# Latent attention steps of a two-layer transformer kernel issued in pairs of opposite order

## The chip, the cores and the metric

One Trainium2 chip, one of its cores. The time is the device time of one execution in microseconds (us). An execution of the kernel before takes 1641.88 us (median of three runs, 1641.62 to 1645.02). Everything is float32 unless a tile is an index, a mask (bfloat16) or a half-precision helper.

## The reference, cut to what matters

Two layers work on 256 latent tokens and 256 context tokens of width 1024. Each layer has three attention branches of eight heads with 64 values each, then a merge through gates, an output projection and a mixture of 16 experts. The change touches the attention alone:

```python
# branch A (global), B (window of +-128 with a sink logit), N (2-D neighbourhood with a bias)
s = q . [k_latent, k_context] * 64 ** -0.5      # (+ band mask in B, + position bias in N)
p = softmax(s)                                  # B adds one sink logit to the sum
o = p . [v_latent, v_context]
# context queries see context keys only, and are needed in layer 0 alone
```

## The kernel before

**Tiles and stages.** A layer projects its normalised tokens to queries, keys and values, runs the attention, merges the three branches through gates, projects, and routes to the experts. The engines have their instruction streams written out by hand and meet through counting semaphores. There is no planner for the attention: the order on each engine is the order in which its loop issues.

**The attention's unit is a pair of heads.** `att_pairs(l)` lists (branch, query tile of 128 tokens, pair of heads), branch outermost and pair innermost: 3 branches x 4 tiles x 4 pairs = 48 in layer 0 (tiles 0 and 1 latent, 2 and 3 context) and 3 x 2 x 4 = 24 in layer 1 (latent only). So layer 0 alternates between 8 latent pairs and 8 context pairs, three times, and layer 1 has 24 latent pairs in a row. A latent pair attends to 512 keys, a context pair to 256. For pair d:

- **S(d), scores** (L2048): for each of the two heads ("sides") one matmul of 64 rows by 128 columns over 512 keys (256 for context), into one of four score banks. The trace records each as two matmuls, and the two sides run side by side on halves of the array's rows.
- **M(d), row maxima** on VectorE, one for each side: L1405 for branch A and for context, L1410 for B (adds the band mask and writes the sum to `probs`), L1417 for latent N (adds the position bias that GpSimd made at L756 from a table that SyncE's queue loads at L612).
- **E(d), exponentials** on ScalarE, one for each side (L1039), into `probs`, a ring of six = three pairs. Each is followed by a short read of the accumulated sum.
- **R(d), reciprocal and normalisation** on VectorE (L1389, L1391).
- **T(d), transposes** on TensorE (L2019): 128x128 blocks of `probs`, four for each side of a latent pair (two for context), into banks 3 and 4.
- **C(d), copies** on ScalarE (L1022) of the transposed blocks to `PT`, which has two buffers (in tiles WK and MB).
- **V(d), values** on TensorE (L2038): `PT` against the values, output tiles of 64 columns, the two sides side by side on halves of the array's columns; 16 recorded matmuls for a latent pair, 8 for a context pair.
- **O(d)** on ScalarE (L1011), after the last of four pairs: copies a query tile's output over its queries.

**Order.** Step s of TensorE's loop (L2007) issues T(s-3), V(s-4), S(s). After the last pair there are four more steps in which the first quarter pieces of the first gate matmul (L2055, two matmuls of 512 columns, four records each) take the place of S; the last step thus ends with V(M-1) and then a gate piece. The merge behind it (L2091 first) begins with a wait for every O. ScalarE's step s (L1005) issues O(s-5), C(s-3), E(s-1); VectorE's step s (L1381) issues R(s-2), M(s). GpSimd's and SyncE's streams do not follow the steps.

**Waits between them.** The ones that matter later:

```python
# T(d): both copies of pair d-1 (banks 3 and 4 are free); its own normalisation, side by side
eng.wait_ge(pt_copied, 2 * p)
# V(d): both copies of its own pair
eng.wait_ge(pt_copied, 2 * p + 2)
# S(d), d >= 2: both exponentials of pair d-2 (its score banks are free)
eng.wait_ge(exp_done, 2 * p - 2)
# C(d): V(d-2) done (PT has two buffers)        E(d): T(d-3) done (probs has three pairs)
eng.wait_ge(pv_mm, p - 1)
eng.wait_ge(pt_tr, 2 * p - 4)
# merge: all O done
eng.wait_ge(o_copied, (M0 + M) // (H // 2))
```

Of the kernel before, what the change touches and what calls it, by code (L numbers as in the profile page):

```python
# [32 lines left out]
CW = 512  # L33
NE = 16
NBIAS = 4
NPROB = 6
# [18 lines left out]
A, B, N = range(NB)  # L55
# [45 lines left out]
def head(b, j, side):  # L101
    return 2 * j + side if b == N else 4 * side + j
# [10 lines left out]
def biased(b, t):  # L113

    return b == B or (b == N and t < NLAT)
# [129 lines left out]
def build(nc, t_in, out):  # L245
# [8 lines left out]
    with ExitStack() as es:  # L254
# [3 lines left out]
        def sem(name):  # L258
# [4 lines left out]
        HT = sb("HT", [P, KD, NT * P])  # L263
# [16 lines left out]
        nmx = sb("nmx", [P, NPROB])  # L280
        psm = sb("psm", [P, NPROB])
# [158 lines left out]
        qk_mm = sem("qk_mm")  # L440
# [435 lines left out]
        def _(eng):  # L876
            act = eng.activation
# [41 lines left out]
            n_sink = 0  # L919
            for l in range(L):  # L920
# [42 lines left out]
                for j, (u, t) in enumerate(jobs):  # L963
                    n = before(proj_jobs, l) + j
                    pb = bank[j % 4]
                    if u in ("kvab", "qa"):
# [3 lines left out]
                        w = P if u == "kvab" else BW  # L970
# [31 lines left out]

                pairs = att_pairs(l)
                M0, M = before(att_pairs, l), len(pairs)
                for s in range(M + 5):  # L1005
                    d = s - 5
                    if 0 <= d < M and pairs[d][2] == H // 2 - 1:
                        b, t, _ = pairs[d]
                        g = (M0 + d) // (H // 2)
                        eng.wait_ge(pv_mm, M0 + d + 1)  # L1010
                        act(qT[b][:, :, P * t:P * t + P], bank[5 + g % 2][:, :].rearrange("p (j q) -> p j q", j=4),  # L1011
                            ACT.Copy).then_inc(o_copied, 1)
                    d = s - 3
                    if 0 <= d < M:
                        b, t, j = pairs[d]
                        p = M0 + d
                        ks = slice(0, NT) if t < NLAT else slice(NLAT, NT)
                        if d >= 2:
                            eng.wait_ge(pv_mm, p - 1)
                        for side in range(2):  # L1020
                            eng.wait_ge(pt_tr, 2 * p + side + 1)
                            act(PT[p % 2][side][:, ks], bank[3 + side][:, :].rearrange("p (k q) -> p k q", k=4)[:, ks],  # L1022
                                ACT.Copy).then_inc(pt_copied, 1)
                    d = s - 1
                    if 0 <= d < M:
                        b, t, j = pairs[d]
                        p = M0 + d
                        w = slice(0 if t < NLAT else SEQ, CW + 1 if b == B else CW)
                        if d >= 3:
                            eng.wait_ge(pt_tr, 2 * p - 4)  # L1030
                        for side in range(2):
                            a = 2 * p + side
                            i = a % NPROB
                            eng.wait_ge(nm_ready, a + 1)
                            src = probs[i] if biased(b, t) else sbank[a % 4]
                            if b == B and side == 0:
                                n_sink += 1
                                eng.wait_ge(sink_put, n_sink)
                            act(probs[i][:, w], src[:, w], ACT.Exp, bias=nmx[:, i:i + 1], scale=1.0 if b == A else -1.0,  # L1039
                                accum_out=psm[:, i:i + 1]).then_inc(exp_done, 1)  # L1040


                for i, (n, half, t) in enumerate(merge_jobs(l)):
# [815 lines left out]
        def _(eng):  # L1859
            mm = eng.matmul  # L1860

            def arrived(key):
                slot, n = landed[key]
                eng.wait_ge(w_in_slot[slot], n)
                return slot
# [75 lines left out]
            for l in range(L):  # L1941
# [64 lines left out]

                pairs = att_pairs(l)  # L2007
                M0, M = before(att_pairs, l), len(pairs)
                for s in range(M + 4):
                    d = s - 3  # L2010
                    if 0 <= d < M:
                        b, t, j = pairs[d]
                        p = M0 + d
                        ks = range(0, NT) if t < NLAT else range(NLAT, NT)
                        eng.wait_ge(pt_copied, 2 * p)
                        for side in range(2):
                            eng.wait_ge(p_norm, 2 * p + side + 1)
                            for k in ks:
                                ins = mm(bank[3 + side][:, P * k:P * k + P],  # L2019
                                         probs[(2 * p + side) % NPROB][:, P * k:P * k + P], ident,  # L2020
                                         start=True, stop=True, is_transpose=True)
                            ins.then_inc(pt_tr, 1)
                    d = s - 4
                    if 0 <= d < M:
                        b, t, j = pairs[d]
                        p = M0 + d
                        g = p // (H // 2)
                        ks = range(0, NT) if t < NLAT else range(NLAT, NT)
                        eng.wait_ge(pt_copied, 2 * p + 2)
                        if j == 0 and g >= 2:  # L2030
                            eng.wait_ge(o_copied, g - 1)
                        for k in ks:
                            for side in range(2):
                                h = head(b, j, side)
                                v = vN[:, k, DH * h:DH * h + DH] if b == N else \
                                    vAB[:, k, b, DH * side:DH * side + DH]
                                dst = bank[5 + g % 2][DH * side:DH * side + DH, P * j:P * j + P]
                                ins = mm(dst, v, PT[p % 2][side][:, k], start=(k == ks[0]), stop=(k == NT - 1))  # L2038
                        ins.then_inc(pv_mm, 1)
                    if s < M:  # L2040
                        b, t, j = pairs[s]
                        p = M0 + s
                        if s >= 2:
                            eng.wait_ge(exp_done, 2 * p - 2)
                        w = slice(0, CW) if t < NLAT else slice(SEQ, CW)
                        for side in range(2):
                            part = slice(DH * side, DH * side + DH)
                            mm(sbank[(2 * p + side) % 4][:, w], qT[b][part, j, P * t:P * t + P],  # L2048
                               kT[b][part, j if b == N else 0, w], start=True, stop=True).then_inc(qk_mm, 1)
                    if s >= M:  # L2050
                        if s == M:
                            wg = arrived(("g00", l))
                            eng.wait_ge(exp_done, 2 * (M0 + M) - 2)
                        for k in range(2 * (s - M), 2 * (s - M) + 2):
                            ins = mm(bank[0][:, :], HT[:, k, 0:P], WR[wg][:, k], start=(k == 0), stop=(k == KD - 1))  # L2055
                        if s == M + 3:
                            ins.then_inc(gate_mm, 1)
                eng.wait_ge(o_copied, (M0 + M) // (H // 2))


# [359 lines left out]
```

## Time and profile before

| | |
|---|---|
| median of three runs | 1641.88 us (1641.62 to 1645.02) |
| the profiled execution | 1642.76 us |
| its span in the profile | 1641.1 us, mean granted TensorE clock 0.982 |
| attention of layer 0, first S to first merge matmul | about 213 to 341 us |
| attention of layer 1 | about 1123 to 1207 us |

In the profile, PE is TensorE's matmuls, PEld its weight loads, DVE VectorE, ACT ScalarE, POOL GpSimd, and L is a line of the kernel. In a timeline neighbouring instructions of one line are merged into one row: start, length and count. Lengths of matmuls overlap (a matmul's record runs to the end of its last output), so the distance from one row's start to the next row's start is the time that the array spent on a block.

### The profile page before, as it was taken

Reading aid. Unit: us, or ns where it says so; the run is one execution under the profiler, and the core shown is the slowest. Engines: PE = TensorE matmul, PEld = TensorE weight load, DVE = VectorE, ACT = ScalarE, POOL = GpSimd, SP = SyncE. Lnnn points to the kernel's source line nnn. Section 1 sums busy time; section 2 is a strip of 40 time slices with the busy share of each in tenths; the row PEclk is TensorE's granted clock in tenths of the full one; section 3 lists DMA queues with packets and bytes.
Section 4 is the critical chain, followed back from the end, with each engine's and each line's share of the span. In section 5 each row is a group of like instructions: output and inputs, shape, how many; then the busy total and the mean of one; then the engine's idle time right before and its main releaser. Section 6 shows DMA issues by size and latency. Waiting matters only on the chain. (4 is left out here: it accounts for less than half of the span.)

```text
span 1641.1 us, 16289 instructions
## 1 busy us (share of the span) xinstructions
PE 1566.8 (95%) x6150; PEld 747.9 (46%) x6150; DVE 662.5 (40%) x1412; ACT 340.4 (21%) x784; POOL 131.0 (8%) x212
## 2 busy tenths in 40 slices
PE   5999999999999999899999979999999998999896
PEld 2444456644444444654444434446654445433332
DVE  2440057776677724611111135404776236111013
ACT  1210078820000021101010014105820011010001
POOL 2000000200000010200100020000200010111110
PEclk9999999999999999899999999999999998999999
DMA  9814420125545460699999796543149748899996
GB/s 349 282 52 139 179 74 2 40 83 168 187 143 194 152 231 39 231 357 368 413 400 427 280 365 245 154 179 116 37 139 362 274 180 305 312 405 403 414 379 274
DMA packets 110640, 382.91 MB, mean 233 GB/s; under 512 B 25051, under 2 KB 29291, under 8 KB 93976
## 3 DMA queue, kind: packets, MB, share of 16 engines
q1 hardware_dynamic: 95520, 328.22, 53.8%
q0 software_dynamic: 14032, 51.24, 8.7%
q10 hardware_dynamic: 1008, 2.38, 0.4%
q8 instruction: 51, 0.84, 0.2%
q14 instruction: 29, 0.24, 0.0%
HBM read 367.53 MB, written 31.52 MB: 243 GB/s over the span
## 5 line engine op out<-in xcount | busy, mean ns | idle before, releaser
L2087 PE MATMUL bank<-ring_sb,HT_sb 128*128 128x512 f32 x544 | 240.1, 594 | 1.1 <-issue 1.1
L1981 PE MATMUL bank<-ring_sb,HT_sb 128*128 128x512 f32 x448 | 200.9, 604 | 3.0 <-ACT HT_sb L911 2.5
L2087 PEld LDWEIGHTS bank<-ring_sb,HT_sb 128*128 128x128 f32 x544 | 102.5, 190 | 133.0 <-issue 132.9
L1204 DVE SCALAR_TENSOR_TENSOR MB_sb<-ring_sb,cT_sb,MB_sb 128x512 f32<-128x512 f32 x192 | 144.3, 752 | 6.8
L1981 PEld LDWEIGHTS bank<-ring_sb,HT_sb 128*128 128x128 f32 x448 | 85.3, 194 | 106.2 <-issue 105.2
L2091 PE MATMUL bank<-ring_sb,QR_sb 128*128 128x512 f32 x288 | 129.5, 592 | 0.0
L2251 PE MATMUL bank<-ring_sb,HT_sb 128*64 128x512 f32 x480 | 106.3, 595 | 0.0
L1978 PE MATMUL bank<-HT_sb,ring_sb 128*128 128x512 f32 (+1 forms) x256 | 97.5, 539 | 0.0
L2269 PE MATMUL bank<-ring_sb,QR_sb 128*128 128x512 f32 x208 | 92.1, 596 | 2.5 <-DMA ring_sb<-w_e_down 2.5
L1405 DVE TENSOR_REDUCE nmx_sb<-bank 128x1 f32<-128x512 f32 (+1 forms) x48 | 26.4, 595 | 163.9 <-PE bank L2048 163.9
L1048 ACT ACTIVATE WK_sb<-bank 128x512 f32<-128x512 f32 x36 | 21.5, 597 | 342.4 <-PE bank L2087 342.3
L2232 PE MATMUL bank<-ring_sb,HT_sb 128*128 128x512 f32 x192 | 85.4, 598 | 2.7 <-ACT HT_sb L1082 2.7
L2091 PEld LDWEIGHTS bank<-ring_sb,QR_sb 128*128 128x128 f32 x288 | 54.7, 190 | 68.9 <-issue 68.9
L2142 PE MATMUL bank<-ring_sb,HT_sb 128*128 128x512 f32 x192 | 84.8, 595 | 0.0
L2241 PE MATMUL bank<-ring_sb,HT_sb 128*128 128x512 f32 x192 | 84.4, 592 | 0.0
L2275 PE MATMUL bank<-ring_sb,QR_sb 128*64 128x512 f32 x304 | 72.4, 619 | 9.5 <-DMA ring_sb<-w_e_down 6.9
L1703 DVE TENSOR_TENSOR QR_sb<-QR_sb,bank 128x512 f32<-128x512 f32 x13 | 13.7, 1057 | 156.1 <-PE bank L2241 90.4
L2048 PE MATMUL bank<-KR_sb,QR_sb 64*128 64x512 f32 (+1 forms) x288 | 70.5, 569 | 4.2 <-ACT MB_sb L1039 3.0
L1705 DVE TENSOR_TENSOR QR_sb<-QR_sb,bank 64x512 f32<-64x512 f32 x19 | 19.8, 1044 | 131.5 <-ACT QR_sb L1095 131.5
L2019 PEld LDWEIGHTS bank<-tab_sb,MB_sb 128*128 128x128 f32 x480 | 51.5, 141 | 44.6 <-issue 42.3
L2019 PE MATMUL bank<-tab_sb,MB_sb 128*128 128x128 f32 x480 | 68.2, 280 | 0.5 <-DVE MB_sb L1391 0.4
L1978 PEld LDWEIGHTS bank<-HT_sb,ring_sb 128*128 128x128 f32 x256 | 48.2, 190 | 45.1 <-issue 43.5
(346 smaller groups left out, 1710.1 us busy)
## 6 DMA issues: line engine op xcount, KB each, us to landing
ring_sb<-w_e_down SPq DMA_DIRECT2D x32, 2048.0 KB, 14.1
ring_sb<-w_mod SPq DMA_DIRECT2D x24, 2048.0 KB, 10.4
ring_sb<-w_in SPq DMA_DIRECT2D x22, 2048.0 KB, 14.5
ring_sb<-w_e_gate SPq DMA_DIRECT2D x16, 2048.0 KB, 11.2
ring_sb<-w_e_up SPq DMA_DIRECT2D x16, 2048.0 KB, 12.0
ring_sb<-w_e_gate SPq DMA_DIRECT2D x22, 1024.0 KB, 13.9
ring_sb<-w_e_up SPq DMA_DIRECT2D x22, 1024.0 KB, 16.3
ring_sb<-w_branch SPq DMA_DIRECT2D x8, 1024.0 KB, 12.2
```

What stands on the lines that cost most here:

```text
L1204: link(stt(a, WR[slot][:, k], cT[:, k, strm:strm + 1], a, ALU.mult, ALU.add))
L1978: ins = mm(bank[j % 4][:, 0:w], WR[slot][:, k, P * t:P * t + P], HT[:, k, 0:w], start=(k == 0), stop=(k == KD - 1))
L1981: ins = mm(bank[j % 4][:, :], HT[:, k, P * t:P * t + P], WR[slot][:, k], start=(k == 0), stop=(k == KD - 1))
L2019: ins = mm(bank[3 + side][:, P * k:P * k + P], probs[(2 * p + side) % NPROB][:, P * k:P * k + P], ident, start=True, stop=True, is_transpo ...
L2087: ins = mm(bank[i % 2][:, :], HT[:, k, P * t:P * t + P], WR[wg][:, k], start=(k == 0), stop=(k == KD - 1))
L2091: ins = mm(bank[2 + i % 2][:, :], qT[n][:, k, P * t:P * t + P], wdown[wb][:, k, CW * half:CW * half + CW], start=(k == 0), stop=(k == 3))
L2142: ins = mm(bank[i % 3][:, :], HT[:, k, P * t:P * t + P], WR[slot][:, k], start=(k == 0), stop=(k == KD - 1))
L2232: ins = mm(bank[0][:, :], hgT[q % 2][:, k], gate[k], start=(k == 0), stop=(k == KD - 1))
L2241: ins = mm(bank[1][:, :], hgT[q % 2][:, k], up[k], start=(k == 0), stop=(k == KD - 1))
L2251: ins = mm(bank[0][HALF * side:HALF * side + HALF, :], hgT[q % 2][:, k, 0:HALF], w[k], start=(k == 0), stop=(k == KD - 1))
L2269: ins = mm(bank[4 + half][:, :], eaT[:, k], w[k][:, CW * half:CW * half + CW], start=(k == 0), stop=(k == 3))
L2275: ins = mm(bank[4][HALF * half:HALF * half + HALF, :], eaT[:, k, 0:HALF], w[k][:, CW * half:CW * half + CW], start=(k == 0), stop=(k == 3))
```

## The change

Only the attention loops of TensorE and ScalarE change. No instruction is added or removed; VectorE's, GpSimd's and SyncE's streams and every semaphore value that is waited for stay. Steps whose pair is latent, and the four steps behind the last pair, are issued two at a time (s even); steps with a context pair keep T(s-3), V(s-4), S(s).

- TensorE, two latent steps: before T(s-3) V(s-4) S(s) T(s-2) V(s-3) S(s+1); after V(s-4) T(s-3) S(s) S(s+1) T(s-2) V(s-3). At the next pair of steps V(s-2) follows V(s-3).
- ScalarE, two latent steps: before C(s-3) E(s-1) C(s-2) E(s), with both sides of E together; after E(s-1) both sides, C(s-3), E(s) side 0, C(s-2), E(s) side 1, then O(s-3) where pair s-3 is the last of four.
- The gate pieces stand where S stands, so the last V(M-1) now follows the last gate piece.

```diff
-                for s in range(M + 4):
-                    d = s - 3        # transposes of d
...
-                    d = s - 4        # values of d
...
-                    if s < M:        # scores of s, or a gate piece
...
+                for s in range(0, M + 4, 2):
+                    if s < M and pairs[s][1] >= NLAT:
+                        for d in (s, s + 1):
+                            if 3 <= d < M + 3:
+                                turned(d - 3)
+                            if d >= 4:
+                                values(d - 4)
+                            scores(d)
+                        continue
+                    if s >= 4:
+                        values(s - 4)
+                    if 3 <= s < M + 3:
+                        turned(s - 3)
+                    scores_or_gate(s)
+                    scores_or_gate(s + 1)
+                    if 2 <= s < M + 2:
+                        turned(s - 2)
+                    if s >= 3:
+                        values(s - 3)
```

`turned`, `values`, `scores` and `first_gate` hold the bodies of the old loop word for word. ScalarE:

```diff
+                for s in range(0, M + 4, 2):
+                    if s < M and pairs[s][1] >= NLAT:
+                        for d in (s, s + 1):
+                            if d >= 3:
+                                copy_turned(d - 3)
+                            weighed(d - 1, 0)
+                            weighed(d - 1, 1)
+                        if pairs[s - 3][2] == H // 2 - 1:
+                            copy_values(s - 3)
+                        continue
+                    if 1 <= s < M + 1:
+                        weighed(s - 1, 0)
+                        weighed(s - 1, 1)
+                    if 3 <= s < M + 3:
+                        copy_turned(s - 3)
+                    if s < M:
+                        weighed(s, 0)
+                    if 2 <= s < M + 2:
+                        copy_turned(s - 2)
+                    if s < M:
+                        weighed(s, 1)
+                    if s >= 3 and pairs[s - 3][2] == H // 2 - 1:
+                        copy_values(s - 3)
```

`weighed` is E of one side, `copy_turned` is C, `copy_values` is O, each with its old waits.

## Rows read from the trace of the kernel before

**Rows 1.** The page: its head and engine shares
```profile
span 1641.1 us, 16289 instructions
...
PE 1566.8 (95%) x6150; PEld 747.9 (46%) x6150; DVE 662.5 (40%) x1412; ACT 340.4 (21%) x784; POOL 131.0 (8%) x212
```

**Rows 2.** Windows: us, then PE, PEld, DVE, ACT, POOL busy, clock, DMA share, GB/s
```profile
213.00:341.00 128.00, 125.88 (x1073) 78.82 (x1074) 93.91 (x294) 105.64 (x304) 15.79 (x35) 1.00 0.13 34
...
1123.00:1207.00 84.00, 82.03 (x690) 51.58 (x690) 57.87 (x155) 65.11 (x154) 14.76 (x27) 1.00 0.20 51
```

**Rows 3.** Waits of PE over the whole span: total us, times, longest
```profile
PE bank L2048 <- ACT MB_sb L1039: 3.0, 2, 1.5
```

**Rows 4.** Timeline of PE, start of layer 0's attention: start us, us, count
```profile
213.07 1.99 PE L2048 MATMUL bank<-KR_sb,QR_sb 64*128 64x512 f32 x8 [0.69 <-ACT QR_sb L987]
216.56 1.13 PE L2048 MATMUL bank<-KR_sb,QR_sb 64*128 64x512 f32 x4 [1.50 <-ACT MB_sb L1039]
217.62 1.09 PE L2019 MATMUL bank<-tab_sb,MB_sb 128*128 128x128 f32 x8
...
221.78 1.13 PE L2048 MATMUL bank<-KR_sb,QR_sb 64*128 64x512 f32 x4
```

**Rows 5.** Timeline of PE, steady latent steps of A, and context blocks
```profile
222.84 1.09 PE L2019 MATMUL bank<-tab_sb,MB_sb 128*128 128x128 f32 x8
223.86 1.09 PE L2038 MATMUL bank<-MB_sb,KR_sb 128*64 128x128 f32 x16
224.88 1.13 PE L2048 MATMUL bank<-KR_sb,QR_sb 64*128 64x512 f32 x4
225.94 1.09 PE L2019 MATMUL bank<-tab_sb,MB_sb 128*128 128x128 f32 x8
...
232.16 1.09 PE L2019 MATMUL bank<-tab_sb,MB_sb 128*128 128x128 f32 x8
...
248.44 0.66 PE L2038 MATMUL bank<-MB_sb,KR_sb 128*64 128x128 f32 x8
```

**Rows 6.** Timeline of ACT and DVE, start of layer 0's attention
```profile
217.63 0.21 ACT L1039 ACTIVATION_READ_ACCUMULATOR MB_sb<-bank,nmx_sb 128x1 f32 x1
217.73 1.28 DVE L1405 TENSOR_REDUCE nmx_sb<-bank 128x1 f32<-128x512 f32 x2
218.31 1.08 ACT L1022 ACTIVATE WK_sb<-bank 128x512 f32<-128x512 f32 x2 [0.47 <-PE bank L2019]
```

**Rows 7.** Timeline, steady step of branch B: maxima and exponentials
```profile
264.31 1.13 PE L2048 MATMUL bank<-KR_sb,QR_sb 64*128 64x512 f32 x4
...
265.58 0.75 DVE L1410 CUSTOM_DVE_ANT_0 MB_sb<-bank,masks_sb,sink_sb 128x512 f32<-128x512 f32 x1 [0.68 <-PE bank L2048]
...
266.26 0.08 DVE L1410 DVE_READ_ACCUMULATOR2_ANT nmx_sb<- 128x1 f32 x1
...
267.10 0.72 ACT L1039 ACTIVATE MB_sb<-MB_sb,nmx_sb 128x513 f32<-128x513 f32 x1
```

**Rows 8.** Timeline of PE, latent B steps behind context steps
```profile
250.84 1.13 PE L2048 MATMUL bank<-KR_sb,QR_sb 64*128 64x512 f32 x4
...
255.31 1.13 PE L2048 MATMUL bank<-KR_sb,QR_sb 64*128 64x512 f32 x4
...
261.21 1.13 PE L2048 MATMUL bank<-KR_sb,QR_sb 64*128 64x512 f32 x4
```

**Rows 9.** Groups by line: the maxima of branch N (busy, mean ns | idle before)
```profile
L1417 DVE CUSTOM_DVE_ANT_1 MB_sb<-bank,WK_sb 128x512 f32<-128x512 f32 x24 | 16.2, 690 | 9.7 <-issue 9.2 <-POOL WK_sb L756 0.4
```

**Rows 10.** Timeline, end of layer 1's attention
```profile
1203.93 1.09 PE L2038 MATMUL bank<-MB_sb,KR_sb 128*64 128x128 f32 x16
1204.95 1.98 PE L2055 MATMUL bank<-ring_sb,HT_sb 128*128 128x512 f32 x4
1205.07 0.60 ACT L1011 ACTIVATE QR_sb<-bank 128x512 f32<-128x512 f32 x1 [3.26 <-PE bank L2038]
...
1206.77 1.45 PE L2091 MATMUL bank<-ring_sb,QR_sb 128*128 128x512 f32 x3
```

More of the change, by code:

```diff
@@ L1004, in _ @@
                 M0, M = before(att_pairs, l), len(pairs)
[L1005 to L1012, printed above, removed]
-                    d = s - 3
[L1014 to L1040, printed above, removed]
@@ new lines, in weighed @@
+                def weighed(d, side):
+                    nonlocal n_sink
+                    b, t, _ = pairs[d]
+                    p = M0 + d
+                    a = 2 * p + side
+                    i = a % NPROB
+                    w = slice(0 if t < NLAT else SEQ, CW + 1 if b == B else CW)
+                    if side == 0 and d >= 3:
+                        eng.wait_ge(pt_tr, 2 * p - 4)
+                    eng.wait_ge(nm_ready, a + 1)
+                    src = probs[i] if biased(b, t) else sbank[a % 4]
+                    if b == B and side == 0:
+                        n_sink += 1
+                        eng.wait_ge(sink_put, n_sink)
+                    act(probs[i][:, w], src[:, w], ACT.Exp, bias=nmx[:, i:i + 1], scale=1.0 if b == A else -1.0,
+                        accum_out=psm[:, i:i + 1]).then_inc(exp_done, 1)
@@ new lines, in copy_turned @@
+                def copy_turned(d):
+                    p = M0 + d
+                    ks = slice(0, NT) if pairs[d][1] < NLAT else slice(NLAT, NT)
+                    if d >= 2:
+                        eng.wait_ge(pv_mm, p - 1)
+                    for side in range(2):
+                        eng.wait_ge(pt_tr, 2 * p + side + 1)
+                        act(PT[p % 2][side][:, ks], bank[3 + side][:, :].rearrange("p (k q) -> p k q", k=4)[:, ks],
+                            ACT.Copy).then_inc(pt_copied, 1)
@@ new lines, in copy_values @@
+                def copy_values(d):
+                    b, t, _ = pairs[d]
+                    g = (M0 + d) // (H // 2)
+                    eng.wait_ge(pv_mm, M0 + d + 1)
+                    act(qT[b][:, :, P * t:P * t + P], bank[5 + g % 2][:, :].rearrange("p (j q) -> p j q", j=4),
+                        ACT.Copy).then_inc(o_copied, 1)
+                for s in range(0, M + 4, 2):
[21 more added lines that the diff above has]
+                        copy_values(s - 3)
@@ L2008, in _ @@
                 M0, M = before(att_pairs, l), len(pairs)
-                for s in range(M + 4):
[L2010 to L2015, printed above, removed]
-                        for side in range(2):
[L2017 to L2022, printed above, removed]
-                    d = s - 4
[L2024 to L2039, printed above, removed]
-                    if s < M:
[L2041 to L2057, printed above, removed]
@@ new lines, in turned @@
+                def turned(d):
+                    p = M0 + d
+                    ks = range(0, NT) if pairs[d][1] < NLAT else range(NLAT, NT)
+                    eng.wait_ge(pt_copied, 2 * p)
+                    for side in range(2):
+                        eng.wait_ge(p_norm, 2 * p + side + 1)
+                        for k in ks:
+                            ins = mm(bank[3 + side][:, P * k:P * k + P],
+                                     probs[(2 * p + side) % NPROB][:, P * k:P * k + P], ident,
+                                     start=True, stop=True, is_transpose=True)
+                        ins.then_inc(pt_tr, 1)
@@ new lines, in values @@
+                def values(d):
+                    b, t, j = pairs[d]
+                    p = M0 + d
+                    g = p // (H // 2)
+                    ks = range(0, NT) if t < NLAT else range(NLAT, NT)
+                    eng.wait_ge(pt_copied, 2 * p + 2)
+                    if j == 0 and g >= 2:
+                        eng.wait_ge(o_copied, g - 1)
+                    for k in ks:
+                        for side in range(2):
+                            h = head(b, j, side)
+                            v = vN[:, k, DH * h:DH * h + DH] if b == N else \
+                                vAB[:, k, b, DH * side:DH * side + DH]
+                            dst = bank[5 + g % 2][DH * side:DH * side + DH, P * j:P * j + P]
+                            ins = mm(dst, v, PT[p % 2][side][:, k], start=(k == ks[0]), stop=(k == NT - 1))
+                    ins.then_inc(pv_mm, 1)
@@ new lines, in scores @@
+                def scores(d):
+                    b, t, j = pairs[d]
+                    p = M0 + d
+                    if d >= 2:
+                        eng.wait_ge(exp_done, 2 * p - 2)
+                    w = slice(0, CW) if t < NLAT else slice(SEQ, CW)
+                    for side in range(2):
+                        part = slice(DH * side, DH * side + DH)
+                        mm(sbank[(2 * p + side) % 4][:, w], qT[b][part, j, P * t:P * t + P],
+                           kT[b][part, j if b == N else 0, w], start=True, stop=True).then_inc(qk_mm, 1)
@@ new lines, in first_gate, with scores_or_gate @@
+                def first_gate(d):
+                    wg = arrived(("g00", l))
+                    if d == 0:
+                        eng.wait_ge(exp_done, 2 * (M0 + M) - 2)
+                    for k in range(2 * d, 2 * d + 2):
+                        ins = mm(bank[0][:, :], HT[:, k, 0:P], WR[wg][:, k], start=(k == 0), stop=(k == KD - 1))
+                    if d == 3:
+                        ins.then_inc(gate_mm, 1)
+                def scores_or_gate(d):
+                    if d < M:
+                        scores(d)
+                    else:
+                        first_gate(d - M)
```

1 line of the change is left out of this document (added).

## The prediction

> **What bounds the kernel now.** I read the page's head first: TensorE's matmuls cover 1566.8 of 1641.1 us [rows 1]. The windows say the same of the two attention stretches that the change touches: PE is busy 125.9 of 128 us and 82.0 of 84 us at a clock of 1.00 (2.4 GHz), with ScalarE at 65 to 106 us and VectorE at 58 to 94 us [rows 2]. In the waits, PE's scores wait for an exponential only twice, 3.0 us in all [rows 3]. So PE sets the time, and what matters is how long its blocks take and whether the new order makes them wait.
>
> The timeline of PE shows the blocks. A steady latent step of branch A is T 1.02 us (222.84 to 223.86), V 1.02, S 1.06: 3.10 us [rows 5]. How much of that is streaming? Two S blocks in one row take 1.99 us where one takes 1.13 [rows 4]: a further S behind an S costs 0.86. A V row of 8 matmuls is 0.66 long and one of 16 is 1.09 [rows 5], so eight more cost 0.43 and a latent V streams in 0.87; T, with the same 1.09, likewise. What is left, 0.15 at T, 0.15 at V and 0.20 at S, is paid wherever the kind of block changes (the forms in the rows differ: 128\*128, 128\*64, 64\*128). That is 0.50 us of each step, the change's target.
>
> **What the change gives.** Two steps keep six blocks, but S follows S and V follows V: one 0.20 and one 0.15 go, **0.35 us for each pair of steps**, 5.85 instead of 6.20. That S behind S streams is in rows 4. V behind V is not shown across a pair boundary; bounds are 0 to 0.15 saved, and I take 0.15, as inside one V block eight tiles stream at the same rate [rows 5]. There are 12 pairs of latent steps in each layer, so 24 x 0.35 = 8.4 us is the most.
>
> Here a rule can be weighed. The Trainium skill (TensorEngine Tiling, Key Properties) says that changing the tiling mode drains TensorE, and (TensorE: Matmul & The Clock Gate, NX overlap) that a drain is 128 cycles, by my estimate 0.05 us at 2.4 GHz. By it the 48 joins would be worth 2.5 us, not 8.4, and the sum below would end near +4.6 us. The rows show three to four times that for a switch, and I go by them.
>
> **What it costs: the start of each layer.** Today S(2) starts at 216.56 when E(0) is done, then T(0), S(3), T(1), V(0), and S(4) at 221.78 [rows 4]. Now S(3) stands before T(0), and it needs E(1), whose last sum is read at 217.84 [rows 6]: S(3) at 217.9, T(0) 1.06 later, 218.96. Its first side is free for the copy 0.69 later (217.62 to 218.31 [rows 4, 6]), 219.65; two copies take 1.08 [rows 6], and V(0), the very next block of PE's order, waits for them until 220.8. Then V 1.02 and T 1.02: S(4) at 222.8 to 222.9, **1.1 us later than today, in each layer**. In steady state V(s-3) lies between T(s-2) and V(s-2) and covers the copy; at the start there is no such V. Behind S(4), layer 0's branch A joins three more times (S, V, S = 0.55). Net **+0.55**.
>
> **Branch B of layer 0, behind context steps.** Seven joins are worth 1.25. But the block that should cover the copy is a context V, 0.44 in stream instead of 0.87, and ScalarE now does E(16) side 0 before C(14). With S(16) at 0: the masked maximum starts at 1.27, is read at 2.03, E takes ScalarE until 2.8 [rows 7], a context copy pair about 0.65 (0.60 of the latent 1.08), so V(14) starts at 3.5 instead of 2.94: 0.55 lost. S(19) behind S(18) wants E(17), whose maximum stands behind R(15) on VectorE: about 0.15 to 0.25. V(16) behind the short V(15) waits for a full copy: 0.4. So S(20), today 10.4 behind S(16) [rows 8], comes 0.4 later; the two remaining pairs return 0.45. Net **-0.05**. Branch N has the same shape; its maxima are a little shorter (0.69 against 0.76 with the read [rows 7, 9]), and today's waits for bias tables there (0.4 us of VectorE's idle [rows 9]) are partly absorbed by the later steps: **-0.4**. Context steps are unchanged.
>
> **Layer 1's steady run.** From S(4) to S(22) there are nine pairs. In branch A, C(s-2) starts at 2.61 behind S(s) (S S 1.92, first side 0.69) and ends at 3.69; V(s-2) is due at 3.86. Free by some 0.1. In branch B E(s) side 0 holds ScalarE until 2.8, so the copies end at 3.87 and V starts at about 3.95: 0.09 late. N is between: 0.03. Sum 2 x 0.35 + 4 x 0.26 + 3 x 0.32 = **-2.7**. VectorE does two maxima (1.28 [rows 6]) and one normalisation in 2.4 us of a step, 4.8 of 5.85, and ScalarE four exponentials and four copies in 4.9 to 5.0, plus 0.5 for an O every other pair: both still fit, with 0.3 us to spare at the fullest. The bias loads hang on the maximum of four sides before; they get 5.85 us for two steps where they had 6.20, and VectorE waited for their tables 0.4 us in all today [rows 9].
>
> **The end of each layer.** Joining the gate pieces and the last V blocks saves about 0.6 in switches (T and the gate have one form, 128\*128). But V(M-1) is now the last block, and the merge waits for every O. Today V starts at 1203.93, its O at 1205.07 for 0.60, and the gate piece from 1204.95 covers it until 1206.77 [rows 10]. Without it the merge's first matmul starts 1.14 + 0.60 + 0.05 = 1.79 behind V's start where a block takes 1.02: **0.77 uncovered**. Layer 1 with its last pair (0.35): -0.35 - 0.6 + 0.77 = **-0.2**. Layer 0, where short context V blocks cost a further 0.2: **+0.4**.
>
> **The sum.** Layer 0: +0.55 - 0.05 - 0.4 + 0.4 = +0.5. Layer 1: +1.1 - 2.7 - 0.2 = -1.8. Together **-1.3 us**, against the profiled execution's 1642.76 (span 1641.1) as well as against the median, 0.9 lower; PE is near full everywhere else, so I pass the shift on whole. Forecast: 1641.88 - 1.3 = **1640.6 us**, -0.08%. A measurement of this kernel can tell about 0.2%, 3.3 us, from no change; this is inside.
>
> No DMA, no VectorE, GpSimd or SyncE instruction is moved. SyncE's table loads and GpSimd's sink copies wait for maxima and transposes that move by under 2.5 us; GpSimd's and VectorE's next work waits for V(M-1), which comes 0.5 us later in layer 0 and some 0.8 earlier in layer 1, under a merge that is PE's.
>
> **Rivals.**
> 1. *Only the switches count*: other engines keep up everywhere. For it: ScalarE and VectorE are busy at most 83% of either stretch [rows 2]. Against: the waits at the start and at the context edges follow from the order alone. It gives 1641.9 - 8.4 = 1633.5; if only half of my waits come true, 1637. Chance 0.18.
> 2. *The copy is late at every V behind V*, which ends slower. Place: C(s-2) on ScalarE, now behind E(s) side 0. My margins there are +0.15 (A) to -0.09 (B), and the boundary occurs 19 times. At 0.3 us more each it costs 5.7: 1640.6 + 5.7 = 1646.3. It decides from (3.3 + 1.3) / 19 = 0.24 us each. Against it: these durations repeat step by step in the trace. Chance 0.08.
> 3. *Weights of a joined block are not loaded under the matmul before.* Weight loads last 747.9 / 6150 = 0.12 us [rows 1]; 41 joins make 5.0 us, and the time 1645.6. Against it: PE and PEld together are 2314 us in a span of 1641 [rows 1], and S behind S shows no gap [rows 4]. Chance 0.03. Beside it: the Trainium skill (TensorE: Matmul & The Clock Gate, What overlaps and what doesn't) says a weight load overlaps running matmuls only in another row group; by that rule this rival holds, but the trace speaks against it.
> 4. My forecast, start and edge waits against the switches: 0.71.
>
> **Numbers.** Range 1637.4 to 1643.6: the main case with its unknowns (waits at the context edges 0.2 to 0.6 each, V behind V, a run-to-run scatter of up to 1 us), and the half-way case of rival 1; the rest of rivals 1 to 3 is outside. Faster by over 0.2%: 0.18; within: 0.71; slower: 0.11.
>
> **What would show it.** In the changed profile: S rows of 8 matmuls 1.99 long and V rows of 32; T to T over two steps of layer 1 in 5.85 (A) to 5.95 (B) us; V(0) starting 1.8 us behind T(0)'s start, with an idle time released by the copy at L1022, in both layers; S(4) 9.8 us behind the first S instead of 8.7; a wait of the first merge matmul for L1011 of about 0.7 us at both ends; layer 0's attention 0.5 longer, layer 1's 1.8 shorter. If pairs take 6.2, joins are worth nothing and the sum fails; if V(0) does not wait, rival 1 is right; if V rows break in the middle with an idle for L1022 in branch A too, rival 2.

## The result

The changed kernel takes 1647.76 us (median of 22 runs, 1643.3 to 1649.88), the kernel before 1641.76 in the same series: ratio **1.0029 with a 95% interval of 1.0022 to 1.0037**. By this ratio it is slower by 4.8 us (by the two medians 6.0). The prediction, 1640.6 with a range of 1637.4 to 1643.6, was wrong.

### The profile after

The page's head and its group of the merge's gate matmuls (busy us, mean ns of one | idle time just before them and what ended it):

```profile
span 1645.7 us, 16289 instructions
...
PE 1565.0 (95%) x6150; PEld 751.9 (46%) x6150; DVE 663.1 (40%) x1412; ACT 339.5 (21%) x784; POOL 132.2 (8%) x212
...
L2141 PE MATMUL bank<-ring_sb,HT_sb 128*128 128x512 f32 x544 | 243.2, 600 | 4.0 <-issue 4.0
```

The span is 4.6 us longer than in [rows 1] while PE is busy 1.8 us *less*. The last row has an idle time of 4.0 us.

The windows of the two attention stretches, with columns as in [rows 2], and the timeline of PE at the start of layer 0 and in layer 1's steady run:

```profile
213.00:341.00 128.00, 123.92 (x1074) 79.49 (x1075) 93.23 (x293) 104.64 (x302) 15.42 (x34) 1.00 0.13 34
1123.00:1207.00 84.00, 80.38 (x693) 52.96 (x693) 58.92 (x156) 64.92 (x154) 15.38 (x28) 1.00 0.20 52
```

```profile
217.80 1.13 PE L2073 MATMUL bank<-KR_sb,QR_sb 64*128 64x512 f32 x4 [0.21 <-ACT MB_sb L1020]
218.86 1.09 PE L2041 MATMUL bank<-tab_sb,MB_sb 128*128 128x128 f32 x8
220.69 1.09 PE L2061 MATMUL bank<-WK_sb,KR_sb 128*64 128x128 f32 x16 [0.74 <-ACT WK_sb L1031]
221.72 1.09 PE L2041 MATMUL bank<-tab_sb,MB_sb 128*128 128x128 f32 x8
222.74 1.56 PE L2073 MATMUL bank<-KR_sb,QR_sb 64*128 64x512 f32 x6
...
1133.30 1.99 PE L2073 MATMUL bank<-KR_sb,QR_sb 64*128 64x512 f32 x8
...
1136.24 1.09 PE L2061 MATMUL bank<-MB_sb,KR_sb 128*64 128x128 f32 x16
1137.17 1.04 PE L2061 MATMUL bank<-WK_sb,KR_sb 128*64 128x128 f32 x16
...
1139.16 1.99 PE L2073 MATMUL bank<-KR_sb,QR_sb 64*128 64x512 f32 x8
```

The attention did nearly what was forecast. S(4) starts 222.74 - 212.98 = 9.76 us behind the first S where it was 8.71 [rows 4]; V(0) waits 0.74 for the copy. Two steps take 5.86 (1133.30 to 1139.16); V to V is 0.93. From the first S to the first merge matmul layer 0 takes 127.34 us against 127.65, layer 1 81.68 against 83.21. Together 1.8 us are gained. Everything between and behind keeps within 0.4, except one stretch: from the first merge matmul of layer 1 to its first output projection it is 129.22 us where it was 123.18, **6.0 us more**. The first output projection before and after:

```profile
1329.95 2.41 PE L2142 MATMUL bank<-ring_sb,HT_sb 128*128 128x512 f32 x5
```

```profile
1334.44 1.98 PE L2196 MATMUL bank<-ring_sb,HT_sb 128*128 128x512 f32 x4
```

Inside this stretch, the timeline of PE at the place of the idle time, before:

```profile
1241.20 1.04 PE L2077 MATMUL bank<-MB_sb,unit_sb 128*2 128x512 f32 x8
1243.37 7.11 PE L2087 MATMUL bank<-ring_sb,HT_sb 128*128 128x512 f32 x16 [1.13 <-issue]
```

and after (timeline with the end of the attention; then windows with the clock, DMA share and GB/s last):

```profile
1203.42 1.09 PE L2061 MATMUL bank<-MB_sb,KR_sb 128*64 128x128 f32 x16
1205.21 3.70 PE L2145 MATMUL bank<-ring_sb,QR_sb 128*128 128x512 f32 x8 [0.70 <-ACT QR_sb L1039]
...
1239.74 1.04 PE L2131 MATMUL bank<-MB_sb,unit_sb 128*2 128x512 f32 x8
1244.80 5.46 PE L2141 MATMUL bank<-ring_sb,HT_sb 128*128 128x512 f32 x6 [4.01 <-issue]
```

```profile
1240.00:1244.00 4.00, 0.79 (x8) 0.00 (x0) 0.61 (x1) 0.00 (x0) 0.50 (x1) 1.00 1.05 387
1244.00:1246.00 2.00, 1.21 (x2) 0.72 (x3) 0.00 (x0) 0.00 (x0) 0.00 (x0) 0.53 1.05 384
1246.00:1248.00 2.00, 2.00 (x3) 0.79 (x3) 0.00 (x0) 0.00 (x0) 0.00 (x0) 0.50 1.05 387
1248.00:1250.00 2.00, 2.00 (x3) 0.67 (x2) 0.00 (x0) 0.00 (x0) 0.00 (x0) 0.50 1.05 387
1250.00:1252.00 2.00, 2.00 (x5) 0.94 (x4) 1.76 (x3) 0.00 (x0) 0.00 (x0) 0.76 1.05 385
```

PE idled 1.13 us ahead of that gate matmul before; now it idles 4.01. The granted clock falls to 0.50 (1.2 GHz) at 1244.1, 0.7 us before PE starts again, and stays there for 6.8 us, with half as many matmuls in each full window. The idle time accounts for 4.0 - 1.1 = 2.9 us, and the part of the slow stretch in which PE works, 1244.8 to 1250.9, for 6.1 / 2 = 3.05: together 6.0, the whole loss.

"Issue" names no releaser, but the code does: this gate matmul waits for its weights. Weights come through a ring of slots, in an order written out by hand on SyncE's queue. In layer 1's merge that order is two tiles of modulation weights (mod7, mod8), then **wb1** (the branch weights of merge n = 1, two transfers of 64 partitions each), then **g10** (the gate weights of n = 1, half 0), then mod9, mod10, g11 and so on. g10's slot held a modulation tile; VectorE frees it by multiplying that tile (L1202 to L1205), and VectorE begins this work when V(M-1) is done (`eng.wait_ge(pv_mm, M0 + M)`, L1420). VectorE's timeline, before and after:

```profile
1205.07 0.48 DVE L1202 TENSOR_SCALAR MB_sb<-ring_sb,cT_sb 128x512 f32<-128x512 f32 x1 [8.37 <-PE bank L2038]
```

```profile
1204.57 0.48 DVE L1226 TENSOR_SCALAR MB_sb<-ring_sb,cT_sb 128x512 f32<-128x512 f32 x1 [10.20 <-PE bank L2061]
```

VectorE starts 1.70 us ahead of the merge's first matmul before (1205.07 against 1206.77 [rows 10]) and 0.65 ahead after (1204.57 against 1205.21). In both, SyncE issues g10 18.43 us behind VectorE's start (at 1223.50 and 1223.00). The rows of that one transfer give its time from issue to landing, before and after:

```profile
L564 SPq DMA_DIRECT2D ring_sb<-w_in x1: 374/374/374, 1223.5 to 1223.5; - x1
...
DMA to landing us min/median/max: 19.8/19.8/19.8
```

```profile
L564 SPq DMA_DIRECT2D ring_sb<-w_in x1: 374/374/374, 1223.0 to 1223.0; - x1
...
DMA to landing us min/median/max: 21.7/21.7/21.7
```

It lands at 1243.28 before and at 1244.71 after, 1.4 us later although PE needs it 1.5 us earlier. A landing is counted in 16 parts: the first comes 34.4 us behind the first merge matmul in both, the last 36.5 before and 39.5 after. PE is ready at 35.5.

### The profile page after: what moved, and what is told of

It is laid out like the page before. It is cut to its first block and busy times, and to the rows that moved or that the text cites. A ratio compares the mean times of both kernels' runs of the same rounds, so it can differ in the third digit from the quotient of the medians.

```text
span 1645.7 us, 16289 instructions
## 1 busy us (share of the span) xinstructions
PE 1565.0 (95%) x6150; PEld 751.9 (46%) x6150; DVE 663.1 (40%) x1412; ACT 339.5 (21%) x784; POOL 132.2 (8%) x212
## 5 line engine op out<-in xcount | busy, mean ns | idle before, releaser
L2073 PE MATMUL bank<-KR_sb,QR_sb 64*128 64x512 f32 (+1 forms) x288 | 65.5, 556 | 4.6 <-ACT MB_sb L1020 3.4
```

## The experiments

Single executions differ by some us in stretches that no edit here touches (the first S of layer 0 starts between 209.7 and 215.1 us in the seventeen traces), so below a time is judged by its interval and a cause by its stretch of the trace. In the diffs, `single(l, s)` says which steps keep the old order, T, V, S.

### Which layer

**e1** keeps the pairs in layer 0 alone, **e2** in layer 1 alone.

```diff
-                    if s < M and pairs[s][1] >= NLAT:
+                    if single(l, s):    # e1: l == 1 or context;  e2: l == 0 or context
```

> Pairs in layer 0 only; layer 1 keeps the old order. Theory (the change's loss is in layer 1's merge, where PE comes to the third gate's weights, g10, 1.5 us earlier while these land 1.4 us later, idles 4.0 us and then runs at half clock for 6.8 us): layer 0's attention 0.3 us shorter, g10's wait about 1 us and no half clock at it, time 0 to 0.5 us below before. Rival 1 (the loss does not belong to layer 1's attention, it is something that any reordering brings, such as another place of the code or of the clock's falls): 3 to 5 us above before, like the whole change.

Measured: 1643.73 us, ratio 1.0002 [0.9993, 1.0011]. Layer 0's attention 127.6, layer 1's 83.21; idle at g10 0.6, no half clock there. Layer 1 is here that of the kernel before, whose trace shows 1.1: single executions of one order differ by that much at this place.

> Pairs in layer 1 only. Theory: all of the loss is here; first scores to first merge matmul 1.5 us shorter, the idle ahead of g10's gate 3 to 4 us instead of 1.1, half clock behind it, time 4 to 5.5 us above before. Rival 1: the loss would be shared with layer 0, 0 to 2 us above before.

Measured: 1648.42 us, 1.0031 [1.002, 1.0043]. Layer 1's attention 81.68; idle 4.4, half clock for 6.8 us, first merge matmul to output projection 129.3. The loss belongs to layer 1's part of the change.

### The order of the two loads

**e3** is the kernel before and **e4** the changed one, each with g10 loaded ahead of wb1 in layer 1.

```diff
+            if half == 0 and l == 1 and n == 1:
+                uses[-2], uses[-1] = uses[-1], uses[-2]
```

> The old order in both layers; in layer 1 alone the weights g10 are asked for one place earlier, ahead of wb1, which is needed 6.9 us later. Theory: PE's idle ahead of g10's gate (1.1 us) goes, wb1 lands in time, 1 to 1.5 us below before. Rival 2 (the wait is not for the order of these two loads, the DMA engines are full there and wb1 becomes late in its place): 0 to 3 us above before.

Measured: 1645.94 us, 1.0017 [1.0003, 1.003]. PE waits 1.7 us for w_branch instead of for g10, with the clock kept; the stretch is 123.8, 0.6 above before. The rival came true: wb1 is late in g10's place. The profiled execution was one of the fastest (1640.8 us), and what the ratio shows beyond the 0.6 us is not seen in it.

> The whole change and the same swap of two loads in layer 1. Theory: no idle and no half clock at the third gate, and the attention's 1.9 us come through: 2.5 to 3.5 us below before, 7 to 8 below the change. Rival 2: wb1 is late instead, time within 2 us of the change. Rival 3 (the clock's fall has nothing to do with this idle): the idle goes, 3 us are won, and the half clock stays, 1 to 2 us above before.

Measured: 1650.99 us, 1.0055 [1.0042, 1.0069]. g10 landed by 1236.3, but the job's first instruction waits for wb1 too, and that now lands last, at 1244.7: 6.8 us of waiting for w_branch, half clock for 6.8 us, 131.6 for the stretch. Rival 2 again, and worse than it said. PE's need is for both tiles at one point, so exchanging them moves the wait to the other.

### Faster branch weights, a trial that turned out otherwise

**e5** (before) and **e6** (changed) load wb1 as four transfers over all 128 partitions instead of two over 64; **e8** adds to e6 the start and end edits of e12 below.

```diff
+                if key == ("wb1", 1):
+                    src = t_in["w_branch"][1, 1].rearrange("(g j d) n -> j g d n", g=2, d=DH)
+                    for j in range(4):
+                        eng.dma_start(wdown[slot][:, j], src[j]).then_inc(w_in_slot[slot], 16)
+                    return
```

> The old order; in layer 1 wb1 is loaded as four transfers over 128 partitions instead of two over 64. In the trace its 4096-byte packets took 316 ns each over 64 partitions, those of wb2 over 128 partitions 159 ns, 512 packets each, so about 5 us of all DMA engines go, and they lie ahead of g10. Theory (PE's idle ahead of the third gate is the landing of g10 behind wb1): g10 lands 4 to 5 us sooner, the 1.1 us idle goes, 1 us below before. Rival (g10 is late for its own late issue, its slot being released by VectorE): idle stays near 1 us, time unchanged.

Measured: 1675.9 us, 1.0201 [1.0187, 1.0215].

> The whole change and the same four wide transfers. Theory: the 4.0 us idle ahead of g10's gate and the 6.8 us of half clock behind it both go, and the attention's 1.9 us come through: 2.5 to 3.5 us below before, 7 to 8 below the change. Rival (the change loses elsewhere too): idle and half clock go, and it still stands above before.

Measured: 1675.77 us, 1.0203 [1.0189, 1.0217].

> The change with the wide transfers, the first four steps of each layer in the old order, and the last values block ahead of the last gate piece. Theory: S(4) again 8.7 us behind the first S (1.1 us back in each layer), no wait of the merge for the last O (0.6 us back in each layer): 3.4 us below the change with wide transfers, 6 to 6.5 below before. Rival (these waits only move to the next block): within 1.5 us of it.

Measured: 1672.37 us, 1.018 [1.0163, 1.0197]. What the edit did is read in SyncE's timeline, a window and PE's waits of e5 (total us, times, longest):

```profile
1216.57 23.53 SPq L563 DMA_DIRECT2D ring_sb<-w_branch  x4
```

```profile
1224.00:1240.00 16.00, 16.00 (x42) 6.87 (x44) 10.86 (x15) 1.19 (x2) 0.00 (x0) 1.00 0.13 54
```

```profile
PE bank L2154 <- issue: 32.6, 1, 32.6
```

The DMA share falls to 0.13, which is 2 of 16 engines, at 54 GB/s where the old form moves 214: the source's outermost dimension is g, of size 2. The queue stands behind it, and g10 comes 32 us late. By the Trainium skill (DMA: Bandwidth & Descriptors, Why a DMA increments its semaphore by 16 and not by 1) a transfer uses the largest number of engines up to 16 that divides the slowest dimension of both sides; the window agrees. These three say nothing for or against a faster wb1. They show that lateness of g10 reaches the end of the kernel in full. The clock falls 2 us behind the start of the idle time and is 0.50 for 34.1 us, of which PE works in the last 3.5 only; two windows of e5:

```profile
1243.00:1273.50 30.50, 0.00 (x0) 0.00 (x0) 0.00 (x0) 0.00 (x0) 0.00 (x0) 0.50 0.62 190
1273.50:1277.10 3.60, 3.52 (x4) 1.51 (x5) 0.00 (x0) 0.00 (x0) 0.00 (x0) 0.50 1.00 347
```

So the half clock costs 3.5 / 2, some 1.8 us, here, and the idle time 32.6 - 1.1 = 31.5: together 33.3, against 33.1 between the medians.

### More traffic in the old order

**e7** is the kernel before with one extra copy of 1 MB from memory to memory behind wb1.

```diff
+                    if key == ("wb1", 1):
+                        eng.dma_start(more_d[:, :], t_in["w_branch"][1, 1, 0:256]).then_inc(w_in_slot[slot], 16)
```

> The old order, and behind wb1 one more transfer of 1 MB within the device memory, waited for with wb1: it doubles nothing of the attention, only what lies ahead of g10. Theory: g10 lands 3 to 5 us later, PE idles 4 to 6 us ahead of its gate, the clock is halved behind it for about 7 us, time 6 to 9 us above before, although the attention is the old one. Rival (the half clock belongs to the new attention order, not to the idle): the idle grows and the clock stays full, 3 to 5 us above.

Measured: 1644.18 us, 1.0011 [1.0002, 1.0021]. g10's last part lands 38.2 us behind the first merge matmul, PE idles 2.8, the clock stays at 1.00, and the stretch is 124.9 (+1.7, which is 2.8 - 1.1). This is a miss: I had expected 4 to 6 us of idle and 6 to 9 us above before. The idle time stayed below that of the change, so the run says that 2.8 us cost themselves and no more at this place; that an idle of 4 us halves the clock with the old order too, it does not say (e15 does).

### Taking the wait away

**e9** (before) and **e10** (changed): g10 ahead of wb1 as in e3, and PE waits for wb1 only ahead of the branch matmul that reads it.

```diff
-                    wb, wg = arrived((f"wb{n}", l)), arrived((f"g{n}{half}", l))
+                    if (l, n) != (1, 1):
+                        arrived((f"wb{n}", l))
+                    wg = arrived((f"g{n}{half}", l))
...
+                    wb = arrived((f"wb{n}", l))
```

> The old order, g10 loaded ahead of wb1 as in the swap, and in layer 1 PE waits for wb1 only ahead of its first branch matmul, 6.9 us behind the gate whose weights are g10 (before, both were waited for ahead of the gate). In the swap g10 landed at 1234.6 and wb1 at 1239.7, both ahead of this need. Theory: no idle at either, 1 us below before. Rival: a later load becomes late in their place, no gain.

Measured: 1640.52 us, 0.9992 [0.9979, 1.0005]; no idle there, stretch 122.0. The interval includes no change, so the 1.2 us that the stretch gains are seen in the trace alone.

> The whole change with the same two edits. With the swap alone g10 landed at 1236.3 and wb1 at 1244.7; PE would now need wb1 at about 1244 to 1246. Theory: idle at most 1 us, no half clock in the merge, the attention's gain comes through: 1.5 to 3 us below before, 6 to 8 below the change. Rival (the change costs elsewhere): idle and half clock gone and still above before.

Measured: 1643.72 us, 1.0007 [0.9993, 1.0022]: by the two ratios 3.6 us below the change, and not the 1.5 to 3 below before that I expected. The idle at g10 and the half clock are gone, but 1.4 us of waiting for a later gate tile stand at 1262, and the stretch is 123.8.

### Undoing the change's start and its end

**e11** is e10 with two more edits in both layers. The start edit leaves the first four steps in the old order (`s < 4` in `single`). The end edit issues V(M-1) ahead of the last gate piece, as in the kernel before:

```diff
+                    if s == M + 2:
+                        values(s - 3)
+                        scores_or_gate(s + 1)
+                        continue
```

> As the last one, with the first four steps of each layer in the old order and the last values block ahead of the last gate piece. Theory: attention about 3.4 us shorter than in the change (1.1 at each start, 0.6 at each end), and if no transfer becomes late 4.5 to 6 us below before. Rival (PE now comes so early that wb1 or a mod row is late again, with half clock behind it): at or above before.

Measured: 1635.87 us, **0.9962 [0.9951, 0.9973]**. Attention 125.65 and 79.94 us, no idle in layer 1's merge, stretch 122.0. It beats both kernels.

**e12** has the start and end edits alone, with the loads as they were.

> The start and end edits of the last one with the loads and waits of before. Theory (what PE gains ahead of g10's landing is lost again there, and the idle, now 5 to 6 us, brings the half clock): attention 3.4 us shorter than in the change, time the same as the change within 1 us, 4 to 6 us above before. Rival (the landing moves with PE): 3 us below the change.

Measured: 1638.33 us, 0.9972 [0.9958, 0.9986]. Attention 125.59 and 79.93, and no idle time, no half clock, stretch 122.1. This is a miss of my expectation: PE came to the merge 1.75 us earlier than in the change, and yet g10 was there. So "PE is early" could not be the cause, and what remained was the order at the end or at the start. Three more runs parted them.

**e13** is the change with the end edit alone; **e14** the change with the start edit alone; **e15** is the old order in every step, with only V(M-1) put behind the last gate piece:

```diff
+                            if d == M + 3:
+                                scores_or_gate(d)
+                                values(d - 4)
+                                continue
```

> The changed kernel with one edit, in both layers: behind the last pair of steps V(M-1) is issued ahead of the last gate piece, as in the kernel before. Theory (the loss sits in the end form: V(M-1) behind the last gate piece starts VectorE's and GpSimd's work of the merge, and with it the release of the slot of g10, some 1.05 us later against PE): VectorE's first operation of layer 1's merge starts 1.7 us ahead of the first merge matmul instead of 0.65; g10's 16 parts land within about 2 us; PE idles at most 1.5 us at that gate, no half clock; attention of layer 1 about 81.0 us; time 1637.5 to 1640, ratio to before about 0.998. Rival (PE is simply early at g10 because the joined steps made attention shorter): PE idles 4 to 5 us there, half clock for 6.8 us, time 1646 to 1649.

Measured: 1640.0 us, 0.9982 [0.9968, 0.9996]. Attention 126.69 and 81.11; no wait at g10 beyond 0.1 us, no half clock.

> The changed kernel with one edit, in both layers: the first four steps keep the old order, so that S(4) comes 8.7 us behind the first S instead of 9.8; the end of each layer is that of the change. Theory (end form): each attention is about 1.1 us shorter than in the change, g10's landing keeps to VectorE, so PE idles 4 to 5.5 us at it and takes half clock for 6.8 us; time 1644 to 1647. Rival (early PE from joined steps): the same idle or more, about the same time; this run does not tell the two apart alone, it says whether the start is worth 1.1 us a layer and whether the gate takes it back.

Measured: 1645.29 us, 1.0016 [1.0001, 1.0032]. Attention 126.29 and 80.62, which is 1.05 and 1.06 below the change; idle 4.3 and half clock as in the change.

> The kernel before with one edit, in both layers: V(M-1) is issued behind the last gate piece, as the change has it, and no step is joined. Theory (end form): VectorE's first operation of layer 1's merge starts about 0.65 us ahead of the first merge matmul, g10 lands later against PE than before by about 1 us, so PE idles 2 to 4 us there, and where it passes some 3 us the clock halves for 6.8 us; from the first merge matmul to the first output projection 124.5 to 129.5 us; time 1643 to 1648. Rival (early PE from joined steps): that stretch stays at 123.2 us, idle about 1.1 us, time 1641 to 1643.

Measured: 1650.49 us, **1.0049 [1.0033, 1.0065]**, above my upper bound. Attention 128.27 and 83.88, and the stretch 129.96. Its timeline of PE and the times of the g10 transfer:

```profile
1205.18 1.09 PE L2069 MATMUL bank<-MB_sb,KR_sb 128*64 128x128 f32 x16
1206.97 3.27 PE L2157 MATMUL bank<-ring_sb,QR_sb 128*128 128x512 f32 x7 [0.70 <-ACT QR_sb L1046]
...
1241.50 1.04 PE L2143 MATMUL bank<-MB_sb,unit_sb 128*2 128x512 f32 x8
1248.29 2.05 PE L2153 MATMUL bank<-ring_sb,HT_sb 128*128 128x512 f32 x2 [5.75 <-issue]
```

```profile
L571 SPq DMA_DIRECT2D ring_sb<-w_in x1: 373/373/373, 1224.8 to 1224.8; - x1
...
DMA to landing us min/median/max: 23.4/23.4/23.4
```

The same of e13:

```profile
1201.43 1.98 PE L2090 MATMUL bank<-ring_sb,HT_sb 128*128 128x512 f32 x4
1203.26 3.60 PE L2157 MATMUL bank<-ring_sb,QR_sb 128*128 128x512 f32 x8
...
1237.68 1.04 PE L2143 MATMUL bank<-MB_sb,unit_sb 128*2 128x512 f32 x8
1238.84 7.11 PE L2153 MATMUL bank<-ring_sb,HT_sb 128*128 128x512 f32 x16
```

```profile
L571 SPq DMA_DIRECT2D ring_sb<-w_in x1: 374/374/374, 1220.0 to 1220.0; - x1
...
DMA to landing us min/median/max: 18.8/18.8/18.8
```

No step is joined in e15 and it has the loss; the steps are joined in e13 as in the change, and it has none. All runs with the old load order line up (us behind layer 1's first merge matmul, from the landing events; PE is ready for g10 at 35.5 in each):

| kernel | V(M-1) | VectorE starts | first, last part of g10 | PE idles | clock |
|---|---|---|---|---|---|
| before | ahead | -1.70 | 34.4, 36.5 | 1.1 | 1.00 |
| e1 | ahead | -1.70 | 34.1, 35.9 | 0.6 | 1.00 |
| e7, extra traffic | ahead | -1.70 | 35.0, 38.2 | 2.8 | 1.00 |
| e12 | ahead | -1.70 | 33.9, 35.4 | 0 | 1.00 |
| e13 | ahead | -1.70 | 34.1, 35.5 | 0.1 | 1.00 |
| change | behind | -0.65 | 34.4, 39.5 | 4.0 | 0.50, 6.8 us |
| e2 | behind | -0.65 | 34.7, 39.9 | 4.4 | 0.50, 6.8 us |
| e14 | behind | -0.65 | 34.4, 39.8 | 4.3 | 0.50, 6.8 us |
| e15 | behind | -0.65 | 35.1, 41.2 | 5.8 | 0.50, 6.8 us |

The 1.05 us by which VectorE starts later explains one part of the lateness. The larger part is that the 16 parts of the landing are 5 to 6 us apart instead of 1.4 to 3.2. Why they spread is **open**. The spread is there one tile earlier (mod8: 4.1 us apart before, 2.7 in e13, 6.6 in the change, 8.4 in e15), while mod7's parts are 1.4 to 1.5 apart in all four, and the DMA engines are full (share 1.0) from then to the landing. It fits that mod7, whose place VectorE frees, is issued 1.06 us later against the merge and mod8, whose place PE frees, only 0.11, so the pause between the two shrinks; but no run changed that alone. GpSimd waits for V(M-1) too, and its small transfers (router weights, bias and norm rows, L758, L683, L686) also start 1.06 us later against the merge; no run parts them from VectorE's work.

## Why the prediction was wrong

**The attention: right in kind, 0.5 us off.** Forecast -1.3, measured -0.3 - 1.5 = -1.8. That the sum came so near is in part luck: layer 0 was 0.8 better than forecast and layer 1 0.3 worse.

- *Switches.* V to V 0.93 in a row instead of 1.02, two steps 5.86 in branch A (forecast 5.85): the 0.35 us for a pair is right, V behind V included. In branch B some of the second V blocks still come 1.01 behind the first, the lateness that the text allowed for. By the drain that the prediction weighs from the Trainium skill (TensorEngine Tiling, Key Properties; TensorE: Matmul & The Clock Gate, NX overlap) two steps would take 6.10 by estimate, and the trace speaks against it for blocks of this size. That its sum, +4.6, is also what the profiles differ by is a coincidence: the loss does not lie in the joins.
- *Start.* +1.06 in both layers (forecast +1.1); e14 measures it by removal: 1.05 and 1.06.
- *Layer 0.* At S(24), behind the seven joins of branch B, the change is 0.5 behind, as the sum had it. At S(32) it is 0.09 behind: the context steps between, which the prediction called unchanged, take 0.4 less. Branch N gained 0.7 (forecast 0.4). So layer 0 is -0.3, not +0.5.
- *Layer 1.* -1.5 against -1.8.
- *End.* O's wait is 0.70 at both ends (forecast 0.77). e15 shows what V(M-1) last costs in the attention by itself: 0.62 and 0.67; e13 gains 0.65 and 0.57 by removing it.

**The step that failed** is "PE is near full everywhere else, so I pass the shift on whole", with its companion, that GpSimd's and VectorE's next work comes "some 0.8 earlier in layer 1, under a merge that is PE's". VectorE did start earlier in absolute time (by 0.5 us), but what counts is its start against PE, and that became 1.05 us later. VectorE's work frees the slot of g10, whose landing PE already waited 1.1 us for in the kernel before; the last part of g10 landed 39.5 us behind the first merge matmul instead of 36.5. Of these 3.0 us VectorE's later start explains 1.05, and why the rest came is open. I had priced V(M-1)'s new place by the one reader that PE waits for at once, O, and not by the others. The price was 6.0 us: 2.9 of idle and 3.05 of halved clock. The sum with it, -1.8 + 6.0 = +4.2, and 0.4 between the layers make the profile's +4.6.

**The rivals.** Rival 1 (1633.5, or 1637 half-way) is wrong about the waits at the start, which are there. Rival 2's copies are late only by tenths. Rival 3 is refuted: the S rows of 8 still take 1.99. My slower rivals looked inside the steps, and the loss came 38 us behind them. The largest single loss, the clock's 3.05 us, had no place in the sum, though an idle time of 1.1 us ahead of a gate piece stood in the trace of before.

**What holds by experiment**: the loss is in layer 1 (e1, e2); it is the place of V(M-1), not the joined steps (e13, e15); the start costs 1.05 a layer (e14); the joins, with both corrected, gain 3.3 us in layer 1's attention and 2.1 in layer 0's and the whole kernel 0.28% (e12), or 0.38% with the two loads and their wait put apart (e11). Between e11 and e12 the intervals overlap, so the edit of the loads is not shown to add anything once V(M-1) is ahead. Shown in part only is the way from V(M-1) to g10: the later start of VectorE and the later landing stand in every trace with V(M-1) last and the old loads, but the spread of the landing is unexplained.

## What to carry to other kernels

When a block moves to the end of a stage, list everyone who waits for it, not only the engine that bounds: here the block's late reader was a vector engine that frees a weight slot, and the bill came 38 us later. Read a stage's arrival *relative* to the side chain: find the waits downstream that are already non-zero (1.1 us here), for they have no slack and pass on the first microsecond of lateness. Such a change is worth trying in parts: the joins alone were a gain, hidden by one block's place.

## What the runs showed of the hardware that I had not expected

- *An idle time has a step in its price.* Idle times of PE of 0.6, 1.1, 1.7 and 2.8 us in this merge cost their own length. In those of 4.0, 4.3, 4.4, 5.8 and 6.8 us the granted clock fell to 0.50 before PE started again and stayed there for 6.8 us; in that of 32.6 for 34.1 us, most of it idle. But 2.8 us is no safe length: among the experts' matmuls of e3 an idle time of 2.57 us was followed by 3.4 us of half clock (2.47 us in e2, 2.68 in e4 and 2.29 in e6 likewise). Timeline and window of e3:

```profile
1541.57 5.35 PE L2339 MATMUL bank<-ring_sb,QR_sb 128*64 128x512 f32 x16 [2.57 <-DMA ring_sb<-w_e_down]
```

```profile
1542.37:1545.77 3.40, 3.40 (x10) 0.97 (x8) 0.00 (x0) 0.00 (x0) 0.00 (x0) 0.50 1.03 426
```

- *A transfer can run at the rate of 2 of the 16 DMA engines* after its dimensions are put in another order: 54 GB/s and a share of 0.13 in e5, 23.5 us of SyncE's queue.
- *A transfer to 64 partitions fills all the engines and moves about half as much.* While wb1 moves in the kernel before, the window has a DMA share of 1.03 and 214 GB/s; around g10's landing it has 1.05 and 387:

```profile
1226.00:1232.00 6.00, 6.00 (x15) 2.66 (x14) 4.73 (x8) 0.60 (x1) 0.00 (x0) 1.00 1.03 214
1240.00:1244.00 4.00, 2.87 (x13) 0.73 (x13) 0.69 (x1) 0.00 (x0) 0.50 (x1) 1.00 1.05 387
```

The Trainium skill (SBUF — State Buffer, Door 1: The DMA port swizzle) says that 64 adjoining partitions reach only 8 of the 16 ports. The rows, 214 against 387 GB/s, agree with about half the rate. What a wb1 over all ports would bring here was not tried, since e5's form of it ran on two engines.
